# Two of eight convolution channel blocks: taps on GpSimd in place of VectorE

## The reference

```
def conformer_conv(u, conv_w, conv_b, ln_w, ln_b):
    a, gt = jnp.split(u, 2, axis=-1)
    y = a * jax.nn.sigmoid(gt)
    y = lax.conv_general_dilated(y, conv_w.astype(y.dtype), window_strides=(1,),
                                 padding=[(CONV_WIDTH - 1, 0)],
                                 dimension_numbers=('NWC', 'WIO', 'NWC'),
                                 feature_group_count=CONV_CH) + conv_b
    y = layer_norm(y, ln_w, ln_b)
    return jax.nn.silu(y)
```

## Time and profile before

| | |
|---|---|
| time, median of 3 runs | 2985.41 us |
| span of the profiled execution | 2982.8 us |
| what lies around the span, by the median | 2.6 us |
| PE, busy | 2965.0 us |
| VectorE, busy | 2538.7 us |
| ScalarE, busy | 2235.4 us |
| GpSimd, busy | 8.3 us |
| the 480 taps with an accumulator (line 184), two layers, busy | 203.1 us |
| the 16 first taps and 16 like them in the normalization (line 192), busy | 11.4 us |

### The profile page before, as it was taken

How to read it: one execution, slowest core, us unless ns; L and a number is a source line. 1 busy time by engine, 2 the same in 40 slices (tenths; PEclk the granted TensorE clock), 3 DMA queues, 4 the chain that set the end, 5 groups by cost and what they waited for, 6 DMA issues and landing times.

```text
span 2982.8 us, 38320 instructions
## 1 busy us (share of the span) xinstructions
PE 2965.0 (99%) x13671; PEld 2478.2 (83%) x13671; DVE 2538.7 (85%) x4060; ACT 2235.4 (75%) x3809; POOL 8.3 (0%) x21
## 2 busy tenths in 40 slices
PE   8999999999999999999999999999999999999998
PEld 7888888878888888888888888888888888888887
DVE  6767679799888799999888888888998998888887
ACT  8798886966778676798885557777669989555684
POOL 0000000000000000000000000000000000000000
PEclk9999999999999999999999999999999999999999
DMA  9655555665556565555665666666565665666565
GB/s 328 194 174 174 173 194 192 202 185 179 176 183 205 164 219 170 175 173 183 183 195 183 204 205 205 210 192 199 153 196 174 184 184 180 190 203 206 181 205 176
DMA packets 305839, 570.35 MB, mean 191 GB/s; under 512 B 18368, under 2 KB 45152, under 8 KB 305264
## 3 DMA queue, kind: packets, MB, share of 16 engines
q1 hardware_dynamic: 301728, 557.65, 59.7%
q10 hardware_dynamic: 3040, 6.42, 0.6%
q0 software_dynamic: 880, 3.83, 0.4%
HBM read 565.73 MB, written 2.10 MB: 190 GB/s over the span
## 4 chain that ended last, share of the span: by engine, by line
PE 95%; ACT 3%; issue 1%; DVE 1%; DMA 0%; DVEq 0%; SPq 0%; ACTq 0%
PE gp L152 84%; PE bk L152 11%; ACT G L167 2%; ACT wh L167 1%; DVE wl L178 0%; DMA raw<-in_w_in 0%; DMA raw<-in_ev_w_mem_kv 0%; PE bk L155 0%; ACT tmp L167 0%; ACT nat L167 0%; DVE merged L231 0%; DVE nat L184 0%; DVE merged L178 0%; DVE nat L178 0%; DVE merged L191 0%
## 5 line engine op out<-in xcount | busy, mean ns | idle before, releaser
L167 ACT ACTIVATE wh<-raw 128x1024 fp32r<-128x1024 f32 (+2 forms) x1138 | 1149.6, 1024 | 584.6 <-PE gp L152 472.1
L178 DVE TENSOR_TENSOR wl<-raw,wh 128x1024 fp32r<-128x1024 f32 (+2 forms) x1138 | 1320.3, 1176 | 298.7 <-ACT wh L167 291.9
L152 PE MATMUL gp<-wh,Hh 128*128 128x512 f32 (+3 forms) x2121 | 822.6, 388 | 0.3 <-DVE wl L178 0.3
L152 PE MATMUL gp<-wh,Hl 128*128 128x512 f32 (+3 forms) x2121 | 814.6, 384 | 0.0
L152 PE MATMUL gp<-wl,Hh 128*128 128x512 f32 (+3 forms) x2121 | 814.6, 384 | 0.0
L152 PE MATMUL gp<-wh,Yh 128*128 128x512 f32 (+2 forms) x1762 | 684.4, 388 | 9.4 <-DVE wl L178 9.4
L152 PE MATMUL gp<-wh,Yl 128*128 128x512 f32 (+2 forms) x1762 | 679.8, 386 | 0.0
L152 PE MATMUL gp<-wl,Yh 128*128 128x512 f32 (+2 forms) x1762 | 679.7, 386 | 0.0
L152 PEld LDWEIGHTS gp<-wh,Hh 128*128 128x128 f32 x2121 | 398.6, 188 | 79.3 <-DVE wl L178 1.4
L152 PEld LDWEIGHTS gp<-wh,Hl 128*128 128x128 f32 x2121 | 398.4, 188 | 78.1
L152 PEld LDWEIGHTS gp<-wl,Hh 128*128 128x128 f32 x2121 | 398.6, 188 | 76.6
(11 more groups left out here) (173 smaller groups left out, 2270.3 us busy)
## 6 DMA issues: line engine op xcount, KB each, us to landing
raw<-in_w_in SPq DMA_DIRECT2D x544, 512.0 KB, 4.2
raw<-in_ev_w_in SPq DMA_DIRECT2D x104, 512.0 KB, 3.8
raw<-in_od_w_in SPq DMA_DIRECT2D x80, 512.0 KB, 3.9
raw<-in_w_out SPq DMA_DIRECT2D x64, 512.0 KB, 5.0
raw<-in_ev_w_out SPq DMA_DIRECT2D x40, 512.0 KB, 4.8
raw<-in_od_w_out SPq DMA_DIRECT2D x36, 512.0 KB, 4.1
raw<-in_w_b_out SPq DMA_DIRECT2D x32, 512.0 KB, 5.0
raw<-in_w_a_out SPq DMA_DIRECT2D x32, 512.0 KB, 4.9
```

What stands on the lines that cost most here:

```text
L152: return self.e.matmul(out, l, r, start=start, stop=stop)
L167: return self.e.activation(out, in_, func, **kw)
L178: return self.sketch(157 + size(a) * 1.042) if self.e is None else self.e.tensor_tensor(out, a, b, op)
```

## The change

The pair of blocks 2 and 3 (`TAPS_BY_POOL`) goes to GpSimd. VectorE multiplies and adds in one instruction; GpSimd takes three: two multiplications of 128x256 (one for each block, each with its own column of weights) into a second buffer, and one addition of 128x512 to the accumulator for both blocks. The bias is added in the multiplication of tap 0, which goes straight to the accumulator. So the pair has 62 multiplications and 30 additions in a layer. The addition waits for its multiplications, and the next tap for the addition. Accumulator and buffer are other columns of `merged`. `tapped` gives the steps behind the taps the signals of both engines to wait for. The planner has two new formulas for GpSimd's instructions.

```diff
--- before.py
+++ after.py
@@ -31,6 +31,7 @@
 END1 = '3a 1b 1a 3b 6 2b *0 7b 2a 4a 5 7a 8 4b'
 END2 = '0a 1a 0b 1b 2 3 *4 6 *5 7'
 BY_DMA = ()
+TAPS_BY_POOL = (2,)
 DUOS = ('gate2', 'gate3', 'out3', 'out2', 'out0', 'ub1_2', 'ub1_3', 'hqk7_1')
 GATE = "0 *1 *2 3 *4 5 *6 7"
 UB0 = "0a 1a 2a 0b 1b 2b 4a 4b *3 6 *5 7"
@@ -175,7 +176,9 @@
             self.table = func
 
     def tensor_tensor(self, out, a, b, op):
-        return self.sketch(157 + size(a) * 1.042) if self.e is None else self.e.tensor_tensor(out, a, b, op)
+        if self.e is None:
+            return self.sketch(200 + size(a) * 2.2 if self.plan.step.engine == "pool" else 157 + size(a) * 1.042)
+        return self.e.tensor_tensor(out, a, b, op)
 
     def scalar_tensor_tensor(self, out, a, s, b, op0, op1, total=None):
         if self.e is None:
@@ -186,7 +189,7 @@
 
     def tensor_scalar(self, out, a, s1, s2, op0, op1=None):
         if self.e is None:
-            return self.sketch(157 + size(a) * 0.8)
+            return self.sketch(200 + size(a) * 0.9 if self.plan.step.engine == "pool" else 157 + size(a) * 0.8)
         if op1 is None:
             return self.e.tensor_scalar(out, a, s1, None, op0)
         return self.e.tensor_scalar(out, a, s1, s2, op0, op1)
@@ -465,6 +468,7 @@
         self.glu = M[:, 0:8 * 286].rearrange("p (c t) -> p c t", t=286)
         self.cv = self.glu[:, :, 30:286]
         self.acc_tap = [M[:, 2304:2560], M[:, 2560:2816]]
+        self.acc_pool, self.tap_pool = (M[:, a:a + 512].rearrange("p (c t) -> p c t", c=2) for a in (2816, 3328))
         self.csq = M[:, 2304:3328].rearrange("p (c t) -> p c t", t=256)
         self.ctwo = M[:, 3584:4096].rearrange("p (c t) -> p c t", t=256)
         self.cvar = [M[:, 3584:3840], M[:, 3840:4096], M[:, 2304:2560]]
@@ -504,7 +508,7 @@
         self.s_gfin = [sig("s_gfin0"), sig("s_gfin1")]
         self.s_m = [sig(f"s_m{n}") for n in range(4)]
         self.s_strict, self.s_ones = sig("s_strict"), sig("s_ones")
-        self.s_cc = sig("s_cc")
+        self.s_cc, self.g_tap = sig("s_cc"), sig("g_tap")
         self.s_out = [sig(f"s_out{i}") for i in range(4)]
         self.g_zero, self.g_halves, self.g_pad = sig("g_zero"), sig("g_halves"), sig("g_pad")
         self.p_mm, self.p_in, self.p_turn = sig("p_mm"), sig("p_in"), sig("p_turn")
@@ -888,6 +892,13 @@
             return [self.v_in.at(("y", 9, 2), ("y", 6, 2))]
         return [self.v_in.at(("y", 13, 2), *(("m", 0, i) for i in range(0, 16, 2)))]
 
+    def tapped(self, l, *cs):
+
+        by = [c for c in cs if c // 2 * 2 in TAPS_BY_POOL]
+        got = [self.g_tap.at(*((l, c // 2 * 2, 30) for c in by))] if by else []
+        rest = [c for c in cs if c not in by]
+        return got + ([self.v_tap.at(*((l, c, 30) for c in rest))] if rest else [])
+
     def sums_of(self, gm):
 
         return self.four[:, 2 * gm.third - 2:2 * gm.third, :] if gm.third else self.gp[gm.g % 2][:, :, :]
@@ -1325,7 +1336,29 @@
             e.wait_ge(*P.p_mm.at(P.outs[1][3].end))
         e.memset(P.glu[:, :, 0:30], 0.0).then_inc(*P.g_pad.up(l))
 
-    return {"zero": zero, "clear_halves": clear_halves, "load_dil": load_dil, "load_constants": load_constants, "load_gfin": load_gfin, "load_second": load_second,
+    def tap(l, c0, k):
+        to = P.acc_pool if not k else P.tap_pool
+        if not k:
+            e.wait_ge(*P.a_glu.at(*((l, c0 // 4, a) for a in range(4))))
+            e.wait_ge(*P.g_pad.at(l))
+            e.wait_ge(*P.s_cc.at(l))
+        before = [b for b in TAPS_BY_POOL if b < c0]
+        if k or before:
+            e.wait_ge(*P.g_tap.at((l, c0, k - 1) if k else (l, before[-1], 30)))
+        for i in range(2):
+            c = c0 + i
+            wk = P.cc[:, 8 * k + c:8 * k + c + 1]
+            bias, add = (P.cc[:, 248 + c:249 + c], ALU.add) if not k else (None, None)
+            x = e.tensor_scalar(to[:, i, :], P.glu[:, c, k:k + 256], wk, bias, ALU.mult, add)
+        if not k:
+            x.then_inc(*P.g_tap.up((l, c0, 0)))
+            return
+        x.then_inc(*P.g_tap.up((l, c0, k, "mult")))
+        e.wait_ge(*P.g_tap.at((l, c0, k, "mult")))
+        out = P.acc_pool if k < 30 else P.cv[:, c0:c0 + 2, :]
+        e.tensor_tensor(out, P.acc_pool, P.tap_pool, ALU.add).then_inc(*P.g_tap.up((l, c0, k)))
+
+    return {"tap": tap, "zero": zero, "clear_halves": clear_halves, "load_dil": load_dil, "load_constants": load_constants, "load_gfin": load_gfin, "load_second": load_second,
             "load_cc": load_cc, "pad": pad, "merge_add": merge_add}
 
 
@@ -2558,8 +2591,9 @@
                     e.wait_ge(*P.a_glu.at(*((l, c0 // 4, a) for a in range(4))))
                     e.wait_ge(*P.g_pad.at(l))
                     e.wait_ge(*P.s_cc.at(l))
-                if c0:
-                    e.wait_ge(*P.v_tap.at((l, c - 2, 30)))
+                before = [b for b in range(0, c0, 2) if b not in TAPS_BY_POOL]
+                if before:
+                    e.wait_ge(*P.v_tap.at((l, before[-1] + i, 30)))
                 e.tensor_scalar(part, src, wk, P.cc[:, 248 + c:249 + c], ALU.mult, ALU.add).then_inc(*P.v_tap.up((l, c, 0)))
             else:
                 e.wait_ge(*P.v_tap.at((l, c, k - 1)))
@@ -2573,13 +2607,15 @@
             m = 4 >> n
             x = e.tensor_tensor(P.csq[:, 0:m, :], P.csq[:, 0:m, :], P.csq[:, m:2 * m, :], ALU.add)
         else:
-            e.wait_ge(*P.v_tap.at(*((l, c, 30) for c in range(8))))
+            for w in P.tapped(l, *range(8)):
+                e.wait_ge(*w)
             x = e.tensor_tensor(P.csq, P.cv[:, 0:4, :], P.cv[:, 4:8, :], ALU.add)
         x.then_inc(*P.v_csum.up((l, "mean", n)))
 
     def center(l, h):
         e.wait_ge(*P.p_mean.at(l))
-        e.wait_ge(*P.v_tap.at(*((l, c, 30) for c in range(4 * h, 4 * h + 4))))
+        for w in P.tapped(l, *range(4 * h, 4 * h + 4)):
+            e.wait_ge(*w)
         x, m = P.cv[:, 4 * h:4 * h + 4, :], P.bank.buf(("mean", l))[:, 0:256].unsqueeze(1).broadcast_to([128, 4, 256])
         e.scalar_tensor_tensor(x, m, -1.0 / 1024, x, ALU.mult, ALU.add).then_inc(*P.v_cent.up((l, h)))
 
@@ -2902,7 +2938,7 @@
             add("act", "glu_move", l, hb, a)
         for c0 in (4 * hb, 4 * hb + 2):
             for k in range(31):
-                add("dve", "tap", l, c0, k)
+                add("pool" if c0 in TAPS_BY_POOL else "dve", "tap", l, c0, k)
         if hb:
             for n in range(3):
                 add("dve", "mean_sum", l, n)
```

## The result

The changed kernel takes 3040.73 us, the median of 4 runs from 3040.26 to 3041.52. The kernel before, run beside it, takes 2985.17 us (2984.69 to 2985.76). The ratio is 1.0186, with a 95% interval from 1.0174 to 1.0198: 55.6 us are lost. The forecast was 3058 us, slower, by turns at SBUF. The sign held, and so did the mechanism for GpSimd's additions; its multiplications held VectorE far less than turns would. Three of the sizes were wrong, and that their errors partly cancel is luck.

The account below looks back on a forecast made before the run. The prediction took PE to bound the kernel, with a matmul in flight for 2965.0 of 2982.8 us. It added 73.0 us of PE standing (36.5 a layer) and 2.6 for the median: 3058.4 us, range 2984 to 3112.

Parts of the forecast that it names:

- turns at SBUF: During GpSimd's taps, each of its 92 instructions a layer lets one VectorE instruction through, 0.640 us each; chance 0.58.
- The gain of 0: Taking 26.1 us a layer of taps off VectorE gives no time back, as PE has no gap there.
- The hold: GpSimd's own instruction time a layer, 49.2 us, during which VectorE is kept out.
- upper bound of 59.8: GpSimd's dearest work a layer: multiplications at 0.329 us, additions at 1.314, scaled from a memset; 59.8 us.
- GpSimd's stage: Time from GpSimd's first tap to its last in a layer: 49.2 + 58.9 = 108.1 us.
- the slack: VectorE's gaps beside GpSimd's work: 58.9 us of its work fill 63.0 us of the earlier schedule.
- The lead: How far VectorE's weight splits are ahead of PE through five buffers: 8.6 us of delay covered.
- What costs nothing: Two more ScalarE table loads, 1.28 us each, fit its idle time behind 1349; without that cover 2.6 us.
- Side by side: Rival: both engines read SBUF together, VectorE's instructions keep their times, 2985.4 us; chance 0.28.
- The pair beside a memset: Two VectorE additions beside GpSimd's memset at 966.24 took 1.29 us, no longer than elsewhere; evidence for unhindered reading.
- GpSimd shut out: Rival: GpSimd works only in VectorE's gaps, its taps come late for the sum, 3017 to 3067 us; chance 0.11.
- The relief: Rival: VectorE's lighter load reaches PE, at most its 17.8 us of idle time, 2968 us; chance 0.03.

Follow-up runs that it names:

- e6_dropped: The changed kernel, but GpSimd fills the sums of its two blocks by one memset instead of computing their taps; 2986.54 us.
- e1_beside: The kernel before, all 248 taps a layer still on VectorE, with GpSimd's 92 instructions a layer added into columns nobody reads; 3039.98 us.

## Why the prediction was right, and which of its sizes were not

**The gain of 0** held: e6_dropped shows it, and e1_beside shows the same loss with all the taps on VectorE.

**The hold** was put at 49.2 us a layer, and is 37.3. The step that failed here is that each engine keeps the other out for the whole of an instruction: it did not hold for the multiplications. And GpSimd's instructions together are dearer than even the upper bound of 59.8: the first multiplications of a layer take 743 ns against at most 329, and an addition 1.28 us, near the upper end of 0.66 to 1.31. Three rows of the changed kernel's timeline, the first two multiplications, the second addition, and VectorE's split beside that addition:

```profile
1023.94 1.49 POOL L195 TENSOR_SCALAR merged<-merged,cc 128x256 f32<-128x256 f32 x2 [57.19 <-ACT merged L168]
...
1034.27 1.28 POOL L181 TENSOR_TENSOR merged<-merged 128x512 f32<-128x512 f32 x1
...
1034.33 2.30 DVE L181 TENSOR_TENSOR wl<-raw,wh 128x1024 fp32r<-128x1024 f32 x1
```

Whole instructions in turn would then hold VectorE for 62 x 0.743 + 30 x 1.28 = 84.5 us. It was held for 37.3: 0.87 us by an addition and 0.15 us by a multiplication, on average. The split above lost 2.30 - 1.22 = 1.08 us of the addition's 1.28, so where the two meet, an addition does come close to a turn. Too low a price and too large a share of it nearly met in the middle, by luck.

**GpSimd's stage** was put at 108.1 us. It ends with the addition at 1167.56 + 1.55 = 1169.11, so it takes 145.2. The multiplications, drawn out to 1556 ns on average, and the waits between the instructions lengthen the stage. It also takes in more of VectorE's gaps, so **the slack** is larger than the 4.1 us of the forecast. Two taps just behind the stage (second), and the same two in the kernel before (first), on VectorE's timeline:

```profile
1140.58 0.88 DVE L184 SCALAR_TENSOR_TENSOR merged<-merged,cc 128x256 f32<-128x256 f32 x2
```

```profile
1170.38 0.86 DVE L187 SCALAR_TENSOR_TENSOR merged<-merged,cc 128x256 f32<-128x256 f32 x2
```

VectorE is 29.8 us late there. With 37.3 us of extra, 7.5 went into gaps. VectorE's busy time (third) up to this place, before and after, gives nearly the same:

```profile
1024.00:1140.58 116.58, 116.58 (x544) 99.94 (x544) 108.00 (x172) 82.27 (x139) 0.00 (x0) 1.00 0.64 200
```

```profile
1024.00:1170.38 146.38, 130.67 (x561) 107.50 (x560) 146.05 (x173) 84.50 (x141) 139.66 (x92) 0.93 0.53 159
```

It is busy 38.1 us longer, and its idle time went from 8.6 to 0.3 us. The forecast had 45.1 us late.

**The lead** of 8.6 us was the other failed step. It was read at one weight buffer of 1024 columns, and it isn't the same everywhere. Where PE last waited, the pieces have 512 columns and PE is through with them in half the time. VectorE's timeline and PE's there, in the kernel before:

```profile
1168.28 1.89 DVE L178 TENSOR_TENSOR wl<-raw,wh 128x512 fp32r<-128x512 f32 x3
```

```profile
1171.14 0.28 PE L152 MATMUL gp<-wh,Hh 128*128 128x256 f32 x1
```

and the same two instructions in the changed kernel:

```profile
1197.55 1.89 DVE L181 TENSOR_TENSOR wl<-raw,wh 128x512 fp32r<-128x512 f32 x3
```

```profile
1198.29 0.38 PE L153 MATMUL gp<-wh,Hh 128*128 128x256 f32 x1 [0.15 <-DVE wl L181]
```

In the kernel before the first of three splits was ready at about 1168.28 + 0.69 = 1168.97 (0.69 is the mean of one split of this shape), 2.2 us before PE came to it. In the changed kernel it is 29.3 us later, and PE waits for it. So PE is 1198.29 - 1171.14 = 27.2 us late, and this stays: the place of the sum moved from 1349.06 to 1376.48, by 27.4. So the lead that counted was this narrow one, and not the one read at a handy place. Attention has little lead as well: its transposed tiles go from VectorE over ScalarE straight to PE, and PE waited 10.2 us for them (`bk <- ACT G` above).

The terms together: 36.5 of the forecast, less 11.9 for the hold, less 3.4 for the slack, and 6.4 more for the lead, are 27.6 us a layer. The runs say 27.8. (The slack is what was left of the hold, so this tests only that the loss is VectorE's lateness of 29.8 less the lead of 2.2.)

**What costs nothing** did: two table loads and the new order behind the taps are within e6_dropped's 1.5 us above the kernel before (ratio 0.9995 to 1.0014).

**The rivals.** Side by side is refuted by VectorE's means. The pair beside a memset, which spoke for it, could not have told: one of its inputs lies in PSUM (`gp` in the earlier trace rows), and the like of it kept its time beside GpSimd's reading too (1214 ns against 1218). GpSimd shut out is refuted by its last addition, which ends at 1169.11, some 207 us ahead of the sum at 1376.48: GpSimd did get in. The relief is refuted by e6_dropped.

**The two rules.** VectorE's split went from 1220 to 1956 ns beside GpSimd's additions, VectorE as a whole lost 0.1 us beside memsets, and the transposes with their single SBUF input kept their time. "SBUF — State Buffer", section "Who interferes with whom", of the Trainium skill draws the line in these three places, and the traces agree with it. They do not show its exclusion for the whole of an instruction in the multiplications, which held VectorE for 0.15 us on average where the first of a layer take 0.74; there the measurement decides. The estimate of 1.12 us for an addition, from "GPSIMD Engine Reference", section 3.1, of the Trainium skill, is a little under the 1.28 us measured.

## What to carry to other kernels

Before work goes to an idle engine, look at what bounds the stretch in which it is to run: where PE was full, a lighter VectorE gave nothing, and a second reader of SBUF beside a nearly full VectorE only took. Price such a reader by its kinds of instruction apart: here an addition of 128x512 held VectorE about six times as long as a multiplication of 128x256, and by element read one and a half times. And take the lead between two engines at its narrowest place in the stretch, not at one buffer.

## What the runs showed of the hardware that was not expected

PE's granted clock fell in GpSimd's stage, which it does in no row. On PE's timeline of the changed kernel:

```profile
1116.03 0.79 PE L153 MATMUL gp<-wh,Hh 128*128 128x512 f32 x1 [6.21 <-DVE wl L181]
1116.62 0.63 PE L153 MATMUL gp<-wl,Hh 128*128 128x512 f32 x1
1117.04 0.63 PE L153 MATMUL gp<-wh,Hl 128*128 128x512 f32 x1
1117.47 0.63 PE L153 MATMUL gp<-wh,Hh 128*128 128x512 f32 x1
```

```profile
1114.00:1124.00 10.00, 7.97 (x23) 6.32 (x24) 9.96 (x10) 1.75 (x5) 9.64 (x6) 0.60 0.48 133
```

PE stood for 6.2 us, and then its matmuls follow each other at 0.43 us instead of 0.227. The stretch's mean of 0.60 says that 8 of its 10 us had the lower level, 1.2 instead of 2.4 GHz. By the rows of the stage, the shortfall is at most 0.03 x 50 + 0.10 x 50 + 0.08 x 45 = 10.1 us in the first layer and 0.10 x 50 + 0.04 x 45 = 6.8 in the second. It is tempting to add this to the loss. But the second layer, with less of it, lost no less (55.6 - 27.4 = 28.2 us), and in the chain of the first only the three pieces at 1043.11, 1044.43 and 1045.71 run at the lower level: 4.6 us for 12 matmuls, of which 1.9 are too many. Elsewhere PE waited for VectorE anyway, and a slower matmul only took the place of a wait. Nor did a slower PE hold VectorE up, which had no gap in these stretches (49.84 and 49.90 of 50 us, 44.93 of 45).

The other surprise is the multiplication: it takes about twice its time on average (means of 1418 to 1673 ns in the runs, 743 when a layer begins), while VectorE beside it loses little. What arbitration does that, the traces don't show.
